# Two-layer decoder step on one Trainium2 core: first gates and products of the channel mixer's sums loaded during the last six spread blocks, four gathered rows between spread and sums

## What is computed

```python
def blk(xb):
    q = (xb @ wq).reshape(PEER_BLOCK, PEER_HEADS, PEER_QDIM)
    s1 = einsum('bhd,nd->bhn', q[..., :half], k1)
    s2 = einsum('bhd,nd->bhn', q[..., half:], k2)
    ...   # top 16 of each half, then the top 16 of their sums: idx, gate
    act = gelu(einsum('bd,bhkd->bhk', xb, u_tab[idx]), approximate=False) * gate
    return einsum('bhk,bhkd->bd', act, v_tab[idx])
```

## Time and profile before

| | us |
|---|---|
| median of 3 runs | 4497.53 (4492.22 to 4514.95) |
| profiled execution, whole | 4511.21 |
| profiled execution, span | 4509.6 |
| TensorE busy | 3870.9 (86%) |
| VectorE busy | 2758.4 (61%) |
| GpSimd busy | 1595.2 (35%) |
| ScalarE busy | 1019.4 (23%) |
| mean rate of the DMA engines | 266 GB/s |

### The profile page before, as it was taken

The page is one execution under the profiler, slowest core; times in us unless marked ns, Lnnn a source line. Parts: engine busy times, 40 slices in busy tenths (PEclk is TensorE's granted clock), DMA queues, the critical chain, the costliest instruction groups (busy, mean ns, idle before and its releaser), DMA issues. The chain is left out here.

```text
span 4509.6 us, 50500 instructions
## 1 busy us (share of the span) xinstructions
PE 3870.9 (86%) x17166; PEld 2874.8 (64%) x17166; DVE 2758.4 (61%) x6096; ACT 1019.4 (23%) x2810; POOL 1595.2 (35%) x1330
## 2 busy tenths in 40 slices
PE   9789958887999889979898688868999799789896
PEld 4578844445877677757676444456777677667675
DVE  0255532222798887757677522345997877667777
ACT  0132211121222355501011112211222555201010
POOL 0011113231054366645555100000352765555553
PEclk9888879898999889989899899968999799899998
DMA  3100157685488899989999564404688999899996
GB/s 125 41 17 14 31 157 205 186 226 172 170 319 320 321 410 417 415 334 388 390 397 401 197 237 146 166 20 151 239 340 305 387 417 417 338 393 387 396 400 264
DMA packets 387503, 1201.42 MB, mean 266 GB/s; under 512 B 34340, under 2 KB 173222, under 8 KB 359278
## 3 DMA queue, kind: packets, MB, share of 16 engines
q0 software_dynamic: 159856, 570.77, 33.4%
q1 hardware_dynamic: 198718, 534.63, 32.8%
q10 hardware_dynamic: 28672, 92.81, 5.3%
HBM read 1108.45 MB, written 85.11 MB: 265 GB/s over the span
## 5 line engine op out<-in xcount | busy, mean ns | idle before, releaser
L2009 POOL DMA_INDIRECT peer_ru<-in_u_rows,peer_expert x512 | 780.4, 1524 | 1767.3 <-DVE peer_expert L2380 857.0
L2133 PE MATMUL peer_bank<-region,peer_v 128*128 128x288 f32 x4096 | 1034.6, 417 | 161.3 <-DMA peer_v<-in_v 117.6
L2133 PEld LDWEIGHTS peer_bank<-region,peer_v 128*128 128x128 f32 x4096 | 800.4, 196 | 395.5 <-DMA peer_v<-in_v 124.3
L2086 PE MATMUL peer_bank<-peer_xT,peer_u 128*128 128x288 f32 x4096 | 1034.4, 410 | 2.6 <-ACT peer_hidden L2209 2.6
L2086 PEld LDWEIGHTS peer_bank<-peer_xT,peer_u 128*128 128x128 f32 x4096 | 777.4, 192 | 210.1 <-issue 4.2
L2299 DVE SCALAR_TENSOR_TENSOR y<-peer_rv,peer_weight,y 128x1024 f32<-128x1024 f32 x512 | 655.9, 1281 | 147.8 <-ACT peer_weight L2157 110.2
L2017 POOL DMA_INDIRECT peer_rv<-in_v_rows,peer_expert x512 | 604.6, 1181 | 253.3 <-issue 140.5
L2309 DVE CUSTOM_DVE_ANT_0 peer_ru<-peer_ru,x 128x1024 f32<-128x1024 f32 x512 | 623.0, 1217 | 36.5 <-DMA peer_ru<-in_u_rows,peer_expert 33.6
L2155 ACT ACTIVATE peer_act_g<-peer_dot 128x1 f32<-128x1 f32 x512 | 103.7, 203 | 1201.2 <-DVE peer_dot L2309 1191.3
L2435 DVE TENSOR_TENSOR region<-region,peer_bank 128x288 f32<-128x288 f32 x496 | 219.6, 450 | 168.7 <-PE peer_bank L2133 161.4
L2106 PE MATMUL peer_bank<-region 128*128 128x128 f32 x1152 | 181.6, 308 | 89.7 <-DVE region L2392 89.7
(11 more groups left out here) (505 smaller groups left out, 4326.5 us busy)
## 6 DMA issues: line engine op xcount, KB each, us to landing
peer_u<-in_uT SPq DMA_DIRECT2D x128, 1024.0 KB
peer_v<-in_v SPq DMA_DIRECT2D x64, 2048.0 KB
mlstm_w_in<-in_w_in_o SPq DMA_DIRECT2D x30, 1792.0 KB, 7.4
mla_keys<-in_keysT SPq DMA_DIRECT2D x256, 144.0 KB, 5.5
scratch_early<-peer_hidden ACTq DMA_DIRECT2D x64, 576.0 KB
scratch_grids<-region ACTq DMA_DIRECT2D x24, 1536.0 KB
region<-scratch_grids SPq DMA_DIRECT2D x32, 1152.0 KB, 27.4
region<-scratch_early SPq DMA_DIRECT2D x64, 576.0 KB
```

The lines of the kernel that those rows point to most:

```text
L2009: pool.indirect_dma_start(ru[:, n % U_ROWS, :], None, u_rows, bass.IndirectOffsetOnAxis(ap=expert[:, T, k:k + 1], axis=0)).then_inc(ru_in[ ...
L2086: mm = mmul(bank[:, UNIT_BANKS[i], 0:TD], u[:, h % URING, i % 2, k, :], xT[:, k, :], start=k == 0, stop=k == KD - 1)
L2133: mm = mmul(bank[:, SUM_BANKS[m % 6], 0:TD], v[:, g % 2, j, c * P:(c + 1) * P], w[:, g % 2, j, :], start=j == 0, stop=j == GI - 1)
```

## The change

The pairs of gates no longer share a place. The first buffer of gates and both buffers of w move into slots 1 to 3 of the `u` ring, which are free once the last unit is done; the second buffer of gates stays in the arena. To free the ring early, the units are shared out over the first 66 blocks: blocks 5 to 65 have one each, blocks 66 to 71 none. SP's list waits first for the units, loads gain and shift, then the products of groups 0 and 1 as their writes land, then eleven of the twelve token blocks of the first gates, then, when the last grid is written, the twelfth, and then the second gates. Four rows that were taken in the sums are taken between the last block and the first multiplication by gates ("gap"); 115 are left for the sums. The order of the loads from group 2 on stays as it was.

```diff
     at |= {("mark", b): 1 + (b % 4 == 3) for b in range(MARKS)}
+    at["gap", 0] = 4
     left = len(PICKS) - sum(at.values())
...
 FRONT = dense_queries()
+
+
+LAST_BLOCKS = 6
 
...
         items.append(("block", b))
-        more = (UNITS - unit) // (MARKS - b)
+        more = (UNITS - unit) // max(1, MARKS - LAST_BLOCKS - b)
         items += [("unit", unit + i) for i in range(more)]
...
         yT = region[:, 0:KD * TD].rearrange("p (k t) -> p k t", k=KD)
-        gates = part([2, NBLK, 2 * GI * BLK])
-        w = part([2, GI, TD])
+        gates = [None, part([NBLK, 2 * GI * BLK])]
 
...
         apart = sb("apart", [P, 2, NK])
+        late = u[:, 1:URING, :, :, :].rearrange("p r a b c -> p (r a b c)")
+        n_w, n_g = 2 * GI * TD, NBLK * 2 * GI * BLK
+        w = late[:, 0:n_w].rearrange("p (a j t) -> p a j t", a=2, j=GI)
+        gates[0] = late[:, n_w:n_w + n_g].rearrange("p (b x) -> p b x", b=NBLK)
         gain, shift = (u[:, 0, i, :, :].rearrange("p a b -> p (a b)") for i in range(2))
...
         spread, kept_g, sent_g = sem("grids_spread"), sem("grids_kept"), [sem(f"grid_sent{i}") for i in range(2)]
-        g_in, h_in = [sem(f"gates_loaded{i}") for i in range(2)], [sem(f"hidden_loaded{i}") for i in range(2)]
+        g_first, g_in, h_in = sem("first_gates_loaded"), [sem(f"gates_loaded{i}") for i in range(2)], [sem(f"hidden_loaded{i}") for i in range(2)]
         weighed, sums, added = sem("weighed"), sem("sums"), sem("sums_added")
...
                         load_v(1)
-                sp.wait_ge(spread, MARKS)
-                for i in range(2):
-                    sp.wait_ge(sent_g[i], 16 * (NBLK // 2))
-                    sp.wait_ge(sent_h[i], 16 * (NGRP // 2))
                 sp.wait_ge(dots, UNITS)
...
                 sp.dma_start(shift, shift_dram.partition_broadcast(P)).then_inc(norm_in, 16)
-                for g in range(NGRP):
-                    if g % 2 == 0:
-                        if g >= 4:
-                            sp.wait_ge(weighed, GI * (g - 2))
-                        sp.dma_start(gates[:, g // 2 % 2, :, :], grids[:, :, g * GI:(g + 2) * GI, :].rearrange("b p c t -> p b (c t)")).then_inc(g_in[g // 2 % 2], 16)
+
+                def load_w(g):
                     if g >= 2:
...
                     sp.dma_start(w[:, g % 2, :, :].rearrange("p a b -> p (a b)"), hidden_dram[g]).then_inc(h_in[g % 2], 16)
-                    if g >= 2:
-                        load_v(g)
+
+                def pair_of_gates(pair, lo, hi):
+                    return gates[pair % 2][:, lo:hi, :], grids[lo:hi, :, pair * 2 * GI:(pair + 1) * 2 * GI, :].rearrange("b p c t -> p b (c t)")
+
+                for i in range(2):
+                    sp.wait_ge(sent_h[i], 16 * (NGRP // 2))
+                    load_w(i)
+                for i in range(2):
+                    sp.wait_ge(sent_g[i], 16 * ((NBLK - i) // 2))
+                sp.dma_start(*pair_of_gates(0, 0, NBLK - 1)).then_inc(g_first, 16)
+                for i in range(2):
+                    sp.wait_ge(sent_g[i], 16 * (NBLK // 2))
+                sp.dma_start(*pair_of_gates(0, NBLK - 1, NBLK)).then_inc(g_in[0], 16)
+                sp.wait_ge(spread, MARKS)
+                sp.dma_start(*pair_of_gates(1, 0, NBLK)).then_inc(g_in[1], 16)
+                for g in range(2, NGRP):
+                    pair = g // 2
+                    if g % 2 == 0 and pair >= 2:
+                        sp.wait_ge(weighed, GI * (g - 2))
+                        sp.dma_start(*pair_of_gates(pair, 0, NBLK)).then_inc(g_in[pair % 2], 16)
+                    load_w(g)
+                    load_v(g)
 
...
                         block(i)
+                gelu_rows(("gap", 0))
                 for m in range(NGRP * KD):
...
                     pair = g // 2
+                    if g == 0:
+                        dve.wait_ge(g_first, 16)
                     dve.wait_ge(g_in[pair % 2], 16 * (pair // 2 + 1))
...
                         at = (g % 2 * GI + j) * BLK
-                        tt(w3, w3, gates[:, pair % 2, :, at:at + BLK], ALU.mult).then_inc(weighed, 1)
+                        tt(w3, w3, gates[pair % 2][:, :, at:at + BLK], ALU.mult).then_inc(weighed, 1)
 
...
                     take_rows(("mark", b))
+                take_rows(("gap", 0))
                 weigh(0)
```

## The result

| | median us | runs | against before |
|---|---|---|---|
| before | 4495.43 | 9 | |
| changed | 4473.13 | 9 | 0.9953 (95%: 0.9934 to 0.9972) |
| before, measured again beside the last experiments | 4494.33 | 23 | |
| changed, beside that one | 4474.27 | 12 | 0.9957 (0.9941 to 0.9973) |

The change saves 20 to 22 us, 0.5%. The forecast was 4473 us. The profiled execution has a span of 4483.0 us. Of all the executions reported here a single one, of `x8_before_gates_then_rows`, ran in a slow state (6015 us), and its ratio is taken without it.

What follows compares the result with a forecast made beforehand. No one engine bounds it; DMA engines are full in spread and sums, with 15.2 us unused between. Between counts of 13.9 and 10.4 us, 12.3 per mixer, 24.6 for both: 4497.5 - 24.6 = 4473 us, range 4456 to 4495.

Steps and rivals of the forecast that it cites:

- Part 1: Spread stage: packing units into 66 blocks only exchanges six blocks without units from front to back, and costs nothing.
- The 6 us per mixer: Last six blocks: at the low TensorE clock each would lose about 1 us, were the spread on the chain.
- Part 2: Before the last grid: 3.9 MB of earlier transfers make it slip by 3 to 9.4 us, 6.5 taken.
- Part 3: Last grid to first gates: about 13.5 us (11 to 17) instead of 23.3; less the slip, 3.3 us earlier per mixer.
- Part 4: Sums: four rows fewer, 4.19 MB at 395 GB/s, save 10.6 us per mixer.
- The second way of counting: Hole between spread and sums: only unused DMA time can be won, 10.4 of 15.2 us per mixer.
- the first one: Count by parts, per mixer: 10.6 us from the sums plus 3.3 from earlier first gates, 13.9 us.
- (a): Loads take it back: slip 9.4 us, gates 3 us later, 7 of 10.6 us return; 4490 us; chance 0.24 with (d).
- (b): Last six blocks: slip only 2 us, gates after 12 us, 20 us saved per mixer; 4458 us; chance 0.18.
- (c): Gap rows starve at 7.7 us each among three queues, 9 us lost per mixer; 4516 us; chance 0.08.
- (d): Last hidden write lands late, so products load only after the last grid; would look like (a); chance 0.24 with (a).

Runs made afterwards that it cites:

- x8_before_gates_then_rows: Kernel before, with four rows taken right behind the first multiplication by gates, units and loads unchanged: 4481.57 us, 0.9976 of before.
- x5_units_packed_only: Kernel before, with only the units packed into the first 66 blocks, loads and rows unchanged: 4490.77 us, 0.9995 of before.
- x3_eight_rows_fewer: Changed kernel with the last 8 of 256 gathered rows of each mixer left out, all out of the sums: 4433.61 us, 0.9868 of before.
- x6_eight_rows_in_gap: Changed kernel with eight rows in the gap instead of four: 4485.34 us, 0.9986 of before.
- The second profile: Profile of the changed kernel run once more, nothing altered, beside the last experiments: 4474.27 us, 0.9957 of before.
- x2_loads_only: Changed kernel without the four rows in the gap, which are back in the sums (119 rows): 4487.16 us, 0.9987 of before.
- x11_table_in_three: Changed kernel with 18 rows in the last four groups, first table in three pieces, gain and shift last, gates before gap rows: 4458.46 us, 0.9926 of before.

## Why the prediction was right, and where two errors cancelled

**Part 1, packing at no cost: right.** `x5_units_packed_only` measures 0.9995. The last six blocks of the changed kernel are this window:

```profile
3835.00:3859.00 24.00, 12.93 (x59) 10.85 (x57) 21.82 (x36) 12.28 (x38) 19.45 (x14) 0.65 1.02 403
```

They take 24.0 us, near VectorE's pace of 23.4. TensorE's granted clock is 0.65 of full, a mixture of the 1.2 and the 2.4 GHz level (it was 0.99 from 3844 to 3881 before). The 6 us per mixer that the prediction priced for the case that the spread is on the chain did not come: in `x5_units_packed_only` these blocks have clocks of 0.66 and 0.69, and its interval ends at 6 us of loss for both mixers together.

**Part 2, a slip of 6.5 us: wrong.** The slip of the last grid is -0.5 and +0.1 us in the first profile, +3.3 and +3.5 in the second. The second pair looks like scatter, since packing alone, without any early load, has +2.8 and -0.4. In the last six blocks, where the loads are issued, the ten kernels that have them take 23.9 to 26.0 us against 23.9 with packing alone. The engines carried no more up to the last grid than before: 366.3 us at 411 GB/s are 150.5 MB, before 366.8 at 410, 150.4 MB. The loads displaced gathers: SP's queue moved 31.0 MB in this stretch and not 28.6, the gathers' queue 92.4 MB and not 95.3. That the five-deep rings of rows took this up is my reading, not shown. The last marking row's dot came 0.4 us after the last grid and not 3.2 before, but 2.7 us of this shift come with the packing alone (`x5_units_packed_only`), so at most 1 us of it can be the loads'.

**Part 3, 13.5 us from last grid to first gates: wrong.** It is 19.7 and 19.8. I had counted the last twelfth and the rows. I had taken the eleven blocks ahead of it as down by then; they need 26 us, where the row before gives a median of 27.4 us for a whole table under load. That row was in my hands and I used only its size. The rows' end was wrong too, and alone would have given the same 19.7 us: their first dot came later than I had counted from, and one pause of 6.8 us stood among them. The sum of parts 2 and 3 came out right because one error was the other's reverse, which is luck: predicted 6.5 + 13.5 = 20.0 us, measured 19.2 and 19.9; the first gates come 4.1 and 3.6 us earlier in the first profile (predicted 3.3), and 0.4 earlier and 0.1 later in the second.

**Part 4, 10.6 us for four rows less: price right, bookkeeping wrong.** A row costs 2.5 us (`x3_eight_rows_fewer`), I had 2.65. But the sums shrank by 8.9 and 3.0 us only, the second time by 6.3 and 2.1. The gathers that the gap rows set free were still in flight when the sums began, so from the first gates on the engines move the same bytes: 116 x 20.9 + 395 x 493.1 + 329 x 65 GB/s us = 218.6 MB before, 309 x 20.8 + 392 x 484.3 + 339 x 65 = 218.3 MB after. The sums are shorter because their first 20 us are no longer empty.

**The second way of counting was the sound one.** It said that only unused DMA time can be won, 10.4 us per mixer. Of the 14.6 us of layer 1, 11.9 were won; two mixers make 24 us, and 20 to 22 were measured. The forecast took 12.3 per mixer, between this count and the first one, whose parts were wrong; that 4473 was hit to the microsecond is luck. And the count has a limit that `x6_eight_rows_in_gap` shows: there hardly more DMA time is unused, and the kernel is 11 to 15 us slower. In the profiled pair 26.6 us lie between the spans, of which 19.6 in the two stretches from first mark to last addition; 4.6 us lie between the first queries and the first marks of the mixers and 2.4 us ahead of layer 0's, where the edit changes nothing, so I don't credit them to it. The second profile gives 8.8 us for the two stretches; the means of eight mixers each, under `x8_before_gates_then_rows`, give 17.

**The rivals.** (a), the loads take it back, rests on a slip of 9.4 us, which no profile shows; its time of 4490 is near that of `x2_loads_only`, for another reason. (b) needs no slip and 12 us to the gates; the slip was nil but not the rest. (c), starved rows, is not seen with four rows: they come 3.24 us apart in the gap, with one pause of 6.8, near the 7.7 of the rival. (d), products loaded too late, is not seen either: they are issued 10 and 20 us ahead of the last grid. What I had not listed is that neither half is worth much alone, 0 and 6 us, and both together 21.

## What to carry to other kernels

Where the DMA engines are full before and after a hole, count the time they stand unused, not the wait you remove: here 12 of 15 us lay behind the wait, in the first group's sums. To fill such a hole, transfers must be in flight when it opens; in the kernel before, the same four rows gave nothing ahead of the gates and about 12 us behind them; with the early loads either order works. Do not go past the fill: eight rows lost much of what four had won, for a reason that stays open. Before shortening a wait further, look for other unused DMA time: the last four groups, bound by TensorE, gave about as much again, merely by sharing out the rows differently.

## What the runs showed of the hardware that I had not expected

A load of 1.08 MB (eleven of twelve blocks of 96 KB) in runs of 768 bytes took 26.1 to 27.5 us to land in full engines (all kernels that load the table in two pieces), and one of 96 KB, issued later on the same queue, 8.0 to 9.9 us. The size of the small one does not set its time: in the changed kernel it landed at 3877.7, 1.5 us behind the large one (3876.2), and in `x11_table_in_three` it took 5.7 us. Loads of 3.9 MB put in front of a full stretch hardly lengthened it (the last six blocks 23.9 to 26.0 us, 23.9 without them); gathers gave way, 92.4 MB and not 95.3 up to the last grid.
